# Sixteen gate chunks moved out of the sliding attention to stand behind it, and a bias store and load moved from SyncE to GpSimd

## What is computed

```python
hn = rms_norm(h, attn_norm_g)
u_raw, v_raw, q, k, v, gate_a, gate_b = split(hn @ w_in)
a = u * spatial(layer_norm(gelu(v_raw)))              # gMLP mixer, chunks of 128
b = swa_sink_attention(q, k, v, attn_sinks, rel_bias)  # window 128, 8 query heads
merged = (sigmoid(gate_a) * (a @ w_proj_a) + sigmoid(gate_b) * (b @ w_proj_b))
h = h + merged @ w_out                                 # then a mixture of experts
```

## Time and profile before

| | us |
|---|---|
| median of 3 runs | 3449.92 (3447.57 to 3478.59) |
| the profiled execution, as a run | 3460.93 |
| its span in the profile | 3459.0 |
| TensorE busy, matmul | 3153.3 (91%) |
| VectorE busy | 2018.1 (58%) |
| ScalarE busy | 1115.6 (32%) |
| GpSimd busy | 209.1 (6%) |
| granted clock of TensorE, mean | 0.91 |

### The profile page before, as it was taken

How to read it: one execution, slowest core, us unless ns; L and a number is a source line. 1 busy time by engine, 2 the same in 40 slices (tenths; PEclk the granted TensorE clock), 3 DMA queues, 4 the chain that set the end, 5 groups by cost and what they waited for, 6 DMA issues and landing times. The chain is left out here.

```text
span 3459.0 us, 37239 instructions
## 1 busy us (share of the span) xinstructions
PE 3153.3 (91%) x13388; PEld 2366.3 (68%) x13388; DVE 2018.1 (58%) x2636; ACT 1115.6 (32%) x1638; POOL 209.1 (6%) x66
## 2 busy tenths in 40 slices
PE   6999899998899998999899998999996787969885
PEld 4888686555488886888686555488875555747774
DVE  5777713553277777777613553377774533557776
ACT  3222222434222123222221435221213323336665
POOL 0000000000000000000000000000000000016663
PEclk8999999766999999999998768999998878989998
DMA  5232122000132222222222000232314201249995
GB/s 152 85 109 97 44 69 60 25 1 1 49 110 97 85 97 86 97 85 97 57 68 49 25 1 1 73 110 85 109 37 97 77 25 49 73 168 333 324 331 209
DMA packets 235202, 324.16 MB, mean 94 GB/s; under 512 B 56256, under 2 KB 203720, under 8 KB 222664
## 3 DMA queue, kind: packets, MB, share of 16 engines
q1 hardware_dynamic: 229896, 312.12, 28.0%
q0 software_dynamic: 4608, 8.40, 0.7%
q10 hardware_dynamic: 576, 2.10, 0.2%
HBM read 316.82 MB, written 14.16 MB: 96 GB/s over the span
## 5 line engine op out<-in xcount | busy, mean ns | idle before, releaser
L1939 DVE SCALAR_TENSOR_TENSOR x_T<-acc,x_T 128x512 f32<-128x512 f32 x352 | 242.9, 691 | 206.1 <-PE acc L909 205.9
L878 PE MATMUL score<-h_hi,gate_hi 128*128 128x512 f32 x704 | 278.6, 396 | 34.2 <-DVE h_lo L1893 29.2
L1919 DVE RECIPROCAL recip_tile<-exp_tile 128x512 f32<-128x512 f32 x88 | 295.1, 3353 | 6.5
L879 PE MATMUL score<-h_lo,gate_hi 128*128 128x512 f32 x704 | 277.4, 394 | 0.0
L880 PE MATMUL score<-h_hi,gate_lo 128*128 128x512 f32 x704 | 277.0, 393 | 0.0
L878 PE MATMUL score<-h_hi,up_hi 128*128 128x512 f32 x704 | 274.0, 389 | 0.2 <-DVE up_lo L1876 0.2
L879 PE MATMUL score<-h_lo,up_hi 128*128 128x512 f32 x704 | 273.9, 389 | 0.0
L880 PE MATMUL score<-h_hi,up_lo 128*128 128x512 f32 x704 | 273.9, 389 | 0.0
L907 PE MATMUL acc<-hid_hi,down_hi 128*128 128x512 f32 x640 | 251.6, 393 | 8.8 <-DVE x_T L1939 8.8
L909 PE MATMUL acc<-hid_hi,down_lo 128*128 128x512 f32 x640 | 251.6, 393 | 0.0
L908 PE MATMUL acc<-hid_lo,down_hi 128*128 128x512 f32 x640 | 251.1, 392 | 0.0
(11 more groups left out here) (375 smaller groups left out, 6636.5 us busy)
## 6 DMA issues: line engine op xcount, KB each, us to landing
weights<-in_ffn_w_gate SPq DMA_DIRECT2D x44, 1024.0 KB, 5.3
weights<-in_ffn_w_up SPq DMA_DIRECT2D x44, 1024.0 KB, 5.4
weights<-in_ffn_w_down SPq DMA_DIRECT2D x44, 1024.0 KB, 5.5
arena<-in_expert_w_gate SPq DMA_DIRECT2D x32, 1024.0 KB, 5.9
arena<-in_expert_w_up SPq DMA_DIRECT2D x32, 1024.0 KB, 6.2
weights<-in_expert_w_down SPq DMA_DIRECT2D x30, 1024.0 KB, 5.7
weights<-in_w_in SPq DMA_DIRECT2D x23, 1024.0 KB, 5.3
weights<-in_w_out SPq DMA_DIRECT2D x12, 1024.0 KB, 5.2
```

Of the source, the lines that this page charges most:

```text
L878: mm(ps, hi[:, kc, cols], h_hi[:, kc, :], start=kc == 0, stop=False, skip_group_check=True)
L879: mm(ps, hi[:, kc, cols], h_lo[:, kc, :], start=False, stop=False, skip_group_check=True)
L1919: V.reciprocal(rt[:, :], et[:, c, :])
L1939: V.scalar_tensor_tensor(x_T[:, c, :], acc[c % 2][:, :], 0.5, x_T[:, c, :], ALU.mult, ALU.add).then_inc(acc_free[c % 2], 1)
```

## The change

Three edits. The gate tickets no longer stand between the units: the list has `sv` and then all sixteen gates, TensorE does them in one block after the last `values`, ScalarE empties them and VectorE splits loads 9 to 16 after its part of the attention. The attention runs one unit further ahead on each engine. The store and load of the relative bias go from SyncE's queue to the front of GpSimd's. An `act.drain()` goes as well.

```diff
                  + [("q", c, 4 + c // 2) for c in range(4)] + [("k", 0, 6), ("vtok", 0, 6)]
-                 + [("gate", c, 7 + c // 2) for c in range(6)]
                  + [("sv", c, None) for c in range(4)]
-                 + [("gate", c, 7 + c // 2) for c in range(6, 16)]
+                 + [("gate", c, 7 + c // 2) for c in range(16)]
...
# SyncE
-                if n == 3:
-
-                    sp.wait_ge(relrow_ready, 1)
-                    sp.dma_start(rel_dram, rrow.unsqueeze(1).broadcast_to([8, P, 384])).then_inc(rel_stored, 16)
-                    sp.wait_ge(rel_stored, 16)
-                    sp.dma_start(bias_t, bass.AP(rel_dram.tensor, 127, [[383, P], [384 * P, 8], [1, 256]])
-                                 ).then_inc(bias_loaded, 16)
...
# TensorE
                 scores(1)
+                scores(2)
                 for n in range(NSW):
-                    if n + 2 < NSW:
-                        scores(n + 2)
+                    if n + 3 < NSW:
+                        scores(n + 3)
                     turns(n)
                     if n == SV_STEP:
                         for i in range(4):
                             spatial(i)
-                    g = n // 2
-                    linear2(T2["gate", g], "gate", g, 7 + g // 2, range(4 * (n % 2), 4 * (n % 2) + 4))
                     if n >= 1:
                         values(n - 1)
                 values(NSW - 1)
+                for g in range(16):
+                    linear2(T2["gate", g], "gate", g, 7 + g // 2)
...
# ScalarE
                 exps(0)
+                exps(1)
                 for n in range(NSW):
-                    if n + 1 < NSW:
-                        exps(n + 1)
+                    if n + 2 < NSW:
+                        exps(n + 2)
                     evac_turn(n)
-                    if n % 2 == 1:
-                        gate_out(n // 2)
...
                 head_out(NSW - 1)
-                act.drain()
+                for g in range(16):
+                    gate_out(g)
...
# VectorE
                 maxima(0)
+                maxima(1)
+                normalize(0)
                 for n in range(NSW):
+                    if n + 2 < NSW:
+                        maxima(n + 2)
                     if n + 1 < NSW:
-                        maxima(n + 1)
-                    normalize(n)
+                        normalize(n + 1)
...
-                    if n % 4 == 3:
-                        split_second(7 + n // 4 + 2)
+                for ld in range(9, 17):
+                    split_second(ld)
                 for c in range(4, 8):
                     ab_low(c)
...
# GpSimd
             pool.sem_inc(ids_free, 1)
+            pool.wait_ge(relrow_ready, 1)
+            pool.dma_start(rel_dram, rrow.unsqueeze(1).broadcast_to([8, P, 384])).then_inc(rel_stored, 16)
+            pool.wait_ge(rel_stored, 16)
+            pool.dma_start(bias_t, bass.AP(rel_dram.tensor, 127, [[383, P], [384 * P, 8], [1, 256]])
+                           ).then_inc(bias_loaded, 16)
             pool.wait_ge(passes_ready, 1)
```

More of the change, by code:

```diff
@@ L1291, in sliding_and_gates @@
                 values(NSW - 1)
+                for g in range(16):
+                    linear2(T2["gate", g], "gate", g, 7 + g // 2)
             for n, (name, i, ld) in enumerate(SEC_T):
+                if name == "gate":
+                    continue
                 if name == "sv":
-                    continue
-                if name == "gate":
                     if i == 0:
@@ L1717, in _ @@
             for n, (name, i, ld) in enumerate(SEC_T):
-                if (name, i) == ("gate", 0):
+                if (name, i) == ("sv", 0):
                     sliding_and_gates()
```

## The result

| | before | changed |
|---|---|---|
| median, 20 runs each | 3473.10 us (3447.46 to 3496.85) | 3457.58 us (3402.66 to 3473.53) |
| ratio | | 0.9888, 95% interval 0.9853 to 0.9923 |
| profiled execution: span, mean clock | 3459.0 us, 0.910 | 3456.6 us, 0.900 |

The ratio leaves out runs more than 1.5% above the fastest of the same kernel; that took no run of the kernel before and 12 of the 20 of the changed one, whose fastest (3402.66) stood alone. The medians of all runs give 3457.58 / 3473.10 = 0.9955. When both were timed again beside later kernels, the ratio was 0.9954 (0.9916 to 0.9992). The change makes the kernel faster, by about half of one per cent, 15 to 20 us.

What follows compares the result with a forecast made beforehand. The prediction took TensorE, 91% busy, as the bound, through its waits and lower clock ahead of `q` and in the sliding attention. Gains of 17.6 + 19.3 = 36.9 us from 3449.92 gave 3413 us, range 3386 to 3437.

Steps and rivals of the forecast that it cites:

- The bias DMAs off SyncE, 17.6 us gained: Ahead of the `q` tickets: loads issued earlier, so `q` starts near 2677.5 and not at 2695.09.
- The two cost each other little: Bias store and `q` loads side by side: 384 GB/s together, 49 GB/s for the store alone, so 17.6 us taken.
- the store holds up the q loads: Rival ahead of `q`: second load up to 17 us late, first gain lost, 3431 us; chance 0.12.
- The lower end, 0: Lower bound of the gain ahead of `q`: loads crawl beside the store and land when they did.
- Slack of the bias: Bias on GpSimd's queue lands near 2676, VectorE needs it at about 2723: some 45 us slack, costed at nothing.
- Start of the attention, 7.4 us: From the end of `vtok` to the first transpose: same order of work, so 7.4 us stays.
- Units at half clock, 78 us, and `spatial` 21.7: Attention units without gates, TensorE the bound at half clock, 2.80 us a wide unit; the `spatial` part stays at 21.7.
- The gate block, 90.3 us: Behind the attention: 32 half tickets at 2.75 us, 88.0 us, plus 2.3 for the first at half clock; loads hidden.
- Sum of the attention stage, 19.3 us gained: End of `vtok` to last gate: 7.4 + 78 + 21.7 + 90.3 = 197.4 us instead of 216.7.
- Behind it, nothing changes: From the last gate to the third `pa` ticket: 7.8 us, order the same, so no change.
- The clock rises by itself: Rival in the attention: VectorE bounds the units at 56 us, 19 to 24 us less, 3389 to 3394; chance 0.15.
- No overlap, 3505 us: Rival in the attention: each unit finishes before the next moves, 170 us instead of 78, slower; chance 0.06.

Runs made afterwards that it cites:

- run 9: The changed kernel as it is, timed again: 3455.14 us, ratio 0.9954 to the kernel before.
- run 3: Changed kernel, bias stored once and copied DRAM to DRAM, 128 copies outermost: first `q` matmul 83.2 us after SyncE issues the spatial weight load.
- run 4: Changed kernel, bias stored once and copied DRAM to DRAM, 8 heads outermost: first `q` matmul 83.1 us after SyncE issues the spatial weight load.
- run 1: Changed kernel with the bias DMAs back on SyncE's queue: last gate 335.6 us after SyncE issues the spatial weight load.
- run 5: Changed kernel with three unused dense matmuls in each of the first 12 attention units: first transpose to last value 93.1 us instead of 99.7.
- run 6: Changed kernel with three gate matmuls in each of the 32 units, twelve gate tickets behind: first transpose to last gate 157.7 us instead of 187.0.
- run 12: Changed kernel with light gates, DRAM-to-DRAM bias copies and one overwritten matmul in each NSA unit: 3333.64 us, ratio 0.9611 to the kernel before.
- run 11: Changed kernel with three gate matmuls in each unit and DRAM-to-DRAM bias copies, timed: 3409.19 us, ratio 0.9831 to the kernel before.
- run 8: Changed kernel with one overwritten matmul in each NSA unit of both layers: S, SyncE's issue of the spatial weight load, at 2533.0 us.

## Why the prediction was right or wrong

The forecast was 36.9 us, a ratio of 0.9893. The ratio of the result, 0.9888, is close to it, but that agreement is luck: by all medians and by the second timing the gain is about 15 to 20 us, and in the stage itself 20.8. The absolute forecast of 3413 us and its range up to 3437 miss the 3457.58 us of the median. Part of that is the base: the three runs shown of before had a median of 3449.92, the twenty 3473.10. The rest, some 21 us, is nearly all one wrong step.

- **The bias DMAs off SyncE, 17.6 us gained: wrong.** It was -1.9 (-0.2 in the profile of run 9). The step that failed is "The two cost each other little", read from the earlier trace rows. In that row the load had been issued 0.75 us ahead of the store. A load issued 2.5 us behind it, with the store now on GpSimd's queue, landed only with the store's end (34.6 us). The prediction had the numbers for this order: it put `relrow_ready` at 2634, and the load was issued at 2637.1. Order and queue changed together, and no run has a load behind a store on SyncE's queue or ahead of one on GpSimd's, so which of the two counts is open. The rival "the store holds up the q loads", at 0.12, is what happened, and one load earlier than I had placed it: the second half of `v`. Why the store leaves the loads 11 GB/s is open; that it does, and that the loss goes with the slow store, is shown (runs 3 and 4). The lower end, 0, was off by 2 us. The sum itself was good once the store was short: 100.7 - 17.6 = 83.1, and run 3 came at 83.2.
- **Slack of the bias: right.** GpSimd's store took 0.9 us longer than SyncE's (from its issue to that of the load 35.6 us against 34.7), the load was issued at 2681.7 and landed in 6.6 us, and VectorE first needed it at 2753.4, 65 us after that. The starved descriptors that the Trainium skill warns of in "SBUF — State Buffer", section "SBUF: two separate sides", do not show here beyond those 0.9 us. It is a weak test: VectorE was busy for 11.23 of the first 18.00 us of the store and for none of the 16.00 us from 2664 to 2680.
- **Start of the attention, 7.4 us: right** (7.9).
- **Units at half clock, 78 us, and `spatial` 21.7: right.** From the first transpose to the last value 99.7 us, of which 21.6 are `spatial`, so 78.1. The 2.80 us of a wide unit, taken from another stage with the same shapes, came as 2.81.
- **The gate block, 90.3 us: 3.0 too long.** The first matmuls were not at half clock; all 384 took 87.3 us.
- **Sum of the attention stage, 19.3 us gained: 21.7**, so right in mechanism and size.
- **Behind it, nothing changes:** up to the last `wo` 1.6 us were given back. Behind the same wait of 2.39 us ahead of the third `pa` ticket, the next matmuls ran at half clock in the changed kernel (1.26 us for three) and at full clock in run 1 (0.79), where nothing was given back.
- **The clock rises by itself: did not happen.** No profile of a kernel with the gates outside and nothing in their place showed it in the attention. TensorE was busy for 41.20 of 41.20 us at 0.50. The simple reading of the Trainium skill, "TensorE: Matmul & The Clock Gate", Part 1, that activity releases the clock, does not agree with this trace if a busy TensorE counts as active. In runs 5 and 6, with three dense matmuls in each unit, the clock was 1.00 there.
- **No overlap, 3505 us: did not happen.** TensorE was busy for 41.20 of 41.20 us, with the engines running one unit further ahead. Whether the old distance would have done was not tried.

Left open: in the profiles of kernels with the gates outside or light, `wo` to the end took 416.6 to 420.5 us, and in the two with the gates between all units 414.4 and 413.9. The expert steps take 20.4 or 21.5 us each, and the changed kernel has more of the longer kind, at a mean clock of 0.96 against 0.98. What decides which kind a step becomes was not tried. Also not tried: a bias store issued on GpSimd's queue just behind the fourth weight load, or only after the `q` loads have landed.

## What to carry to other kernels

Before two transfers are put beside each other, look at which was issued first in the row that says they get along; moving a slow store to another queue frees the queue, but here the loads then waited for its end all the same (34.6 us instead of 5.9), and only a shorter transfer gained anything. Dense work between thin matmuls is worth more than the gaps it fills, because TensorE's clock was 1.00 with it and 0.50 without: taking all of it out saved the stalls and paid with the clock, and leaving in a quarter of it kept both gains. When a busy TensorE shows 0.50, one cheap dense matmul in each unit is worth a try, even one whose result is thrown away.

## What the runs showed of the hardware that I had not expected

- The spread between runs of one kernel came in the main from TensorE's clock in the two NSA stages of the first model: with one added matmul a unit the clock there was 0.94 and 0.97 instead of 0.75 and 0.80, and the spread of six runs fell from 33.6 to 6.4 us (run 12 against run 11). Between the changed kernel's two profiles and run 8, S came 43 and 73 us earlier, for 144 matmuls more.
- The granted clock did not follow busy time: 41.20 of 41.20 us busy at 0.50 in the changed kernel, and 28.00 of 28.00 at 1.00 with three dense matmuls in each unit (run 6).
- 1.5 MB read from 8 partitions of SBUF took 34 us from either queue, 1.5 MB read from DRAM with the same destination 10.5 us (128 copies outside) to 13.6 us (8 heads outside). A load of 1 MB landed after 34.6 us behind the first on GpSimd's queue, after 10.6 and 5.8 us beside the other two, and after 5.4 us (median) elsewhere.
